# Lower parts of the streamed weights on VectorE instead of GpSimd during a selective scan

## The reference

```python
y_diag = jnp.einsum('bclgn,bcsgn,bgrcls,bcsgrp->bclgrp', Cm, Bm, lmat, x)
states = jnp.einsum('bclgn,bgrcl,bclgrp->bcgrpn', Bm, decay_states, x)
states = jnp.einsum('bgrzc,bcgrpn->bzgrpn', decay_chunk, states)
y_off = jnp.einsum('bclgn,bcgrpn,bgrcl->bclgrp', Cm, prev_states, jnp.exp(a_cum))
```

## Time and profile before

| | us |
|---|---|
| three runs: lowest, median, highest | 2100.3, 2104.06, 2104.97 |
| the profiled execution | 2098.91 |
| its span, first to last instruction | 2097.2 |
| TensorE busy | 1942.2 (93%) |
| GpSimd busy | 961.4 (46%) |
| VectorE busy | 816.4 (39%) |
| ScalarE busy | 705.8 (34%) |
| L697, lower parts on GpSimd, 212 times | 533.7 |
| L943, upper parts on ScalarE, 212 times | 223.9 |

### The profile page before, as it was taken

One profiled execution on the slowest core, in us unless ns is written; L12 is line 12 of the kernel. 1 busy time (PEld: TensorE's weight loads), 2 busy tenths in 40 slices (PEclk: granted clock), 3 DMA queues, 4 the chain that ended last, 5 costly groups with the idle time before them and its releaser, 6 DMA issues. The chain is left out here.

```text
span 2097.2 us, 36461 instructions
## 1 busy us (share of the span) xinstructions
PE 1942.2 (93%) x14668; PEld 1773.5 (85%) x14668; DVE 816.4 (39%) x1567; ACT 705.8 (34%) x1292; POOL 961.4 (46%) x685
## 2 busy tenths in 40 slices
PE   7998899988888998999999999899978899999996
PEld 5987887867778998999998998755548899999996
DVE  7364573746455220022233112378655521012134
ACT  4453553634134221122223131266533322122222
POOL 2445454444447643356444342454403565346552
PEclk9998999989998999999999999799999899999998
DMA  4211312113131226332221333420161122222221
GB/s 163 80 51 41 121 51 111 51 70 127 41 117 62 80 72 172 90 121 82 81 79 51 127 136 109 173 78 1 41 222 41 51 81 90 81 81 80 82 82 64
DMA packets 61077, 185.12 MB, mean 88 GB/s; under 512 B 15519, under 2 KB 20287, under 8 KB 59425
## 3 DMA queue, kind: packets, MB, share of 16 engines
q1 hardware_dynamic: 48720, 130.18, 18.9%
q0 software_dynamic: 9952, 50.08, 6.7%
q10 hardware_dynamic: 2288, 3.23, 0.4%
HBM read 167.05 MB, written 27.35 MB: 93 GB/s over the span
## 5 line engine op out<-in xcount | busy, mean ns | idle before, releaser
L1299 PE MATMUL dense<-xs,split 128*128 128x288 f32 x6848 | 978.3, 301 | 28.2 <-POOL xs L805 8.5
L1299 PEld LDWEIGHTS dense<-xs,split 128*128 128x128 f32 x6848 | 942.0, 192 | 63.2 <-issue 43.5
L697 POOL TENSOR_TENSOR split<-ring,split 128x1024 fp32r<-128x1024 f32 x212 | 533.7, 2518 | 815.7 <-ACT split L943 793.7
L943 ACT ACTIVATE split<-ring 128x1024 fp32r<-128x1024 f32 x212 | 223.9, 1056 | 798.2 <-PE dense L1299 775.4
L1299 PE MATMUL dense<-hid,split 128*128 128x288 f32 x3072 | 415.8, 298 | 5.8 <-POOL split L697 5.8
L1299 PEld LDWEIGHTS dense<-hid,split 128*128 128x128 f32 x3072 | 414.3, 191 | 6.0 <-POOL split L697 6.0
L1863 DVE SCALAR_TENSOR_TENSOR tile<-tile,dense 128x576 f32<-128x576 f32 (+1 forms) x56 | 42.2, 754 | 422.0 <-PE dense L1299 422.0
L2032 DVE TENSOR_SCALAR sq<-dense 128x576 f32<-128x576 f32 x64 | 48.5, 757 | 310.5 <-PE dense L1299 310.5
L914 POOL TENSOR_SCALAR tile<-tile,tile,tile 128x128 f32<-128x128 f32 (+3 forms) x128 | 77.8, 622 | 80.8 <-DVE tile L2195 80.8
L1851 DVE SCALAR_TENSOR_TENSOR tile<-tile,tile,tile 128x512 f32<-128x512 f32 x72 | 87.5, 1215 | 41.2 <-ACT tile L1024 39.4
L816 POOL TENSOR_TENSOR hid<-sq,hid 128x576 f32 x64 | 77.3, 1208 | 0.0
(11 more groups left out here) (316 smaller groups left out, 2118.2 us busy)
## 6 DMA issues: line engine op xcount, KB each, us to landing
ring<-in_w SPq DMA_DIRECT2D x212, 512.0 KB, 3.3
tile<-in_state POOLq DMA_DIRECT2D x4, 2048.0 KB, 9.2
o_sssm<-tile POOLq DMA_DIRECT2D x4, 2048.0 KB, 7.5
tile<-in_cmp POOLq DMA_DIRECT2D x32, 256.0 KB, 3.2
tile<-in_win POOLq DMA_DIRECT2D x8, 1024.0 KB, 5.9
tile<-in_sel SPq DMA_DIRECT2D x32, 256.0 KB, 5.2
o_kv<-tile POOLq DMA_DIRECT2D x1, 3456.0 KB, 12.2
bskew<-bscr SPq DMA_DIRECT2D x1, 3072.0 KB, 22.3
```

Of the source, the lines that this page charges most:

```text
L697: pool.tensor_tensor(split[:, j, 1, :], ring[:, j, :], split[:, j, 0, :].bitcast(F32), ALU.subtract).then_inc(w_split, 1)
L943: act.activation(split[:, j, 0, :], ring[:, j, :], ACT.Copy).then_inc(w_hi, 1)
L1299: mm = pe.matmul(dense[:, 2 * par + h_, 0:HT], split[:, j, w, cols], v[:, kk, h_ * HT:(h_ + 1) * HT], start=kk == 0 and t == 0, stop=kk == ...
```

## The change

In the scan's twenty tiles VectorE makes the lower parts that GpSimd made, 38 of them (slots 12 to 49); before and after the scan GpSimd still makes them. The part for the even slot plus 2 is made behind the convolutions, the norm and the residual and ahead of the wait for `y_done`; the one for the odd slot plus 2 is made in the next tile, behind the masked product L1914 (after the last tile for the last one). VectorE waits once for the twelve parts that GpSimd has made, and GpSimd waits for VectorE's last one before it goes on with parts of its own.

```diff
 # GpSimd, loop over the tiles
                 if n + 1 < len(TILES):
                     segment_rows(*TILES[n + 1])
-                if filler(g, c):
-                    split_lo(filler(g, c)[0] + 2)
                 if c == 3:
...
                     if g + 1 < MG:
                         load_states(g + 1)
-                if filler(g, c):
-                    split_lo(filler(g, c)[1] + 2)
             pool.dma_start(a["o_pssm"], st.rearrange("p g m -> p (g m)")).then_inc(outs, 16)
...
+            pool.wait_ge(w_split, S_OUT[1] + 2)
             finish_los(0)
 # VectorE
+            def split_lo(s):
+                if s == GB + 2:
+                    dve.wait_ge(w_split, s)
+                dve.wait_ge(w_hi, s + 1)
+                j = s % NSLOT
+                dve.tensor_tensor(split[:, j, 1, :], ring[:, j, :], split[:, j, 0, :].bitcast(F32),
+                                  ALU.subtract).then_inc(w_split, 1)
+
+            def split_before(n):
+                if n and filler(*TILES[n - 1][:2]):
+                    split_lo(filler(*TILES[n - 1][:2])[1] + 2)
+
             for g, c, n in TILES:
...
                 dve.tensor_tensor(Gm[0:L, 0:L], bM[0:L, P:P + L], triu[0:L, c // 4, 0:L], ALU.mult
                                   ).then_inc(g_masked, 1)
+                split_before(n)
                 dve.wait_ge(g_masked, n + 1)
...
                     residual(B_OUT[0], 2 * c - 2, ALPHA, filler(g, c)[0] + 1)
+                if filler(g, c):
+                    split_lo(filler(g, c)[0] + 2)
 
                 dve.wait_ge(y_done, n + 1)
...
+            split_before(len(TILES))
             mean_square(MG - 1)
             norm(MG - 1)
```

## The result

The changed kernel took 2066.52 us (median of 4 runs, 2065.07 to 2073.3) beside 2102.18 us for the kernel before (4 runs, 2097.8 to 2104.97): a ratio of 0.9839, 95% interval 0.9818 to 0.9861. It is faster by 35.7 us.

A forecast was written before the change was run, and what follows sets the result against it. TensorE, 93% busy, was taken to wait in the scan for a VectorE chain that GpSimd's lower part lengthened. Terms: 18.6 us of waits plus 6.4 of clock, 25.0, so 2079 us; range 2067 to 2094.

The forecast's parts named there:

- rival B: Scan: the long L1851 isn't the split's doing, VectorE's subtraction just adds to its chain; 12.5 us slower, 2116.5; chance 0.09.
- VectorE's price: Each of the 38 lower parts in the scan takes VectorE 1.22 us, 46 us in sum.
- rival C: Scan: VectorE needs 2.4 us per lower part too; only 4.8 us gained, no clock, 2099 us; chance 0.05.
- Rival A: GpSimd's remaining L687, L688, L756 run earlier and delay the even convolution 1 us; 12.6 us gained, 2091; chance 0.16.
- no L1851 above 2 us: Sign that the forecast is right: no such long convolution step remains anywhere in the scan.
- Six state-add waits: TensorE's ordinary waits for L1957 ahead of the next tile shrink from 2.2 to about 0.6 us: 9.6 us gained.
- Two norm tiles: Their L1957 waits (1.65 us): about 1.5 saved, split costs 1.22; taken as 0, between -1 and +1 us.
- Tiles 16 and 0: Shorter waits of TensorE there, 1.81 and 1.04 us before: about 1.5 and 0.8 us gained.
- L730: Tiles 5, 10, 15: without the odd part ahead, two TensorE waits vanish, the third falls to 2.8: 4.6 us gained.
- L1909: Tiles 17 and 18: TensorE's 3.72 us wait behind the four slow L1898 shrinks; 2.1 us go.
- Last chunks: Tiles 4, 9, 14, 19: even part on the path to L1962 against a shorter L1944; 0, 2 us either side.
- The clock: Tiles 2, 3, 8, 12 regain the clock lost after 2.2 us waits in front: 6.4 us, or 0, or more.

The follow-up runs named there:

- e3: Changed kernel plus two unused GpSimd multiplications that read SBUF, at the even part's old place in all tiles but the last chunks: 2097.29 us, ratio 0.9975.
- e4: Changed kernel plus four unused GpSimd memsets that only write SBUF, at that same old place of the even part: 2069.22 us, ratio 0.9843.
- e9: As e8, with GpSimd's wait for the stored states and the load of the next ones moved behind L730: 2050.57 us, ratio 0.9755.
- e8: Changed kernel with the even part back on GpSimd, behind y's gate (in last chunks behind the eight products); odd part stays on VectorE: 2071.81 us, ratio 0.9843.
- e2: Changed kernel with the even part back on GpSimd at its old place, only the odd part on VectorE: 2093.41 us, ratio 0.9966.

## Why the prediction was right or wrong

**The bound and the mechanism were right.** TensorE did wait for a VectorE chain that the lower part lengthened without being waited for by name. e3 put a reader back and lost the gain, e4 put a writer back and kept it. That settles rival B (the long convolution step has another cause): in tile 1 the second step is 0.75 us with nothing else done to it, and nothing in the result ends on B's side.

**VectorE's price was right:** 1.22 us; 38 parts took 49.0 us in sum, 1.29 each, where 46 were forecast. So rival C is out. Rival A (GpSimd's remaining work in place of the split) is real but mostly covered. The decays times mask (L1919, now L1933) take 36.8 us in sum instead of 26.8. One step of the even convolution is above 2 us (2.82 at 219.70, in tile 5), and two of the odd one are, 2.38 each, in tiles 6 and 11. Yet in the six ordinary tiles the even convolution still waits for ScalarE, 0.57 to 1.70 us, so the slack that was put at 0.4 held. Thus the test "no L1851 above 2 us" was too strict. The prediction also says that the long L1851 and L697 end together; by the earlier trace rows L1851 ends 0.55 us later (130.76 and 130.21), within the 0.75 us that such a step takes by itself.

**The waits, term by term.** Forecast were 18.6 us; idle time fell by 20.0.

- Six state-add waits: 2.22 to 0.38 each, 11.1 us instead of 9.6. The chain was costed with durations where starts count: three pairs take 2.83 us, not 3.0, and the subtraction 1.14, not 1.22.
- Two norm tiles (8 and 13): taken as 0 with a bound of 1 us each way, they wait 2.55 and 2.60 instead of 1.65, near the lower bound. VectorE's part was about right: in tile 13 the multiplies go from 4.56 to 3.00 us with 1.22 behind them. What the sum left out is ScalarE, whose decays the chain hangs on. Its table load ahead of them starts 3.86 us behind the end of the last block (408.64 before, 390.30 after) in both kernels, while TensorE now begins the tile 1.86 us sooner behind that end (before, then after):

```profile
410.87 0.63 PE L1406 MATMUL bXM<-ident,tile 128*128 128x128 f32 x4 [2.23 <-DVE tile L1957]
412.50 1.28 ACT L1071 ACT_TABLE_LOAD   x1
```

```profile
390.67 0.63 PE L1403 MATMUL bXM<-ident,tile 128*128 128x128 f32 x4 [0.37 <-DVE tile L1973]
394.15 1.28 ACT L1068 ACT_TABLE_LOAD   x1
```

  So part of what is saved in front of the tile comes back at its end: from the tile's first matmul to the end of the state add the chain grows from 21.0 to 21.9 us, at a clock of 1.00 in both. In tile 8 it shrinks, from 22.6 to 21.9, but TensorE's own work shrinks more, from 21.10 to 19.53, by the clock.
- Tiles 16 and 0: both waits went whole, 1.81 and 1.04, instead of 1.5 and 0.8.
- L730: 7.4 to 4.8, 2.6 us instead of 4.6. Tile 10's wait (0.66) went, but tile 5's only fell from 1.63 to 1.24, and tile 15's from 5.12 to 3.58, not to 2.8. GpSimd stood longer for the store of the states, 9.34 us instead of 7.43 in tile 5 and 7.34 instead of 6.58 in tile 15. The store was taken as fixed; it varies (in the second profile of the changed kernel tile 5 has 8.35 us, and a wait of 0.23), and e8 shows how far.
- L1909 (now L1922): 4.4 to 2.2, as forecast.
- Last chunks: taken as 0 with 2 us to either side, they gave 3.2 us, 10.7 to 7.5. The two state adds of tile 4 now run back to back, and L1960, which was L1944, has its 0.48 us:

```profile
191.32 0.48 DVE L1960 TENSOR_TENSOR tile<-tile,tile 128x256 f32<-128x256 f32 x1
...
192.91 1.28 DVE L1978 TENSOR_TENSOR tile<-bXM,tile 128x512 f32<-128x512 f32 x2
```

- Not in the sum: waits for the squares grew by 1.6; two smaller ones gave 1.6.

**The clock is the term that was mis-sized:** 6.4 us forecast, 13.7 measured. The four tiles named (2, 3, 8, 12) gave 6.4 to the tenth, each now at 1.00. But tile 9 gave 3.0 more, tile 18 2.6 (19.55 instead of 22.11) and tile 19 1.5. The step that failed is the rule that only a 2.2 us wait in front of a tile costs clock, with the last chunks left as an unpriced "or more". These three have their waits inside: L1909 in tile 18 went from 3.72 to 1.57 us and the clock from 0.87 to 1.00; the state loop in tile 9 was waited for 2.00 us instead of 2.79, and the clock went from 0.76 to 0.84, though the wait in front of that tile grew (2.55 against 1.65). The price was right and the list of places too short. (The rule's counterexamples were misread too: the waits of 2.23 us without a loss stand in front of tiles 7 and 13; tile 6 has 0.94.)

How far this goes, the second profile of the changed kernel tells. There tiles 2, 3, 8, 12, 18 and 19 are at 1.00 again, with the same busy times to 0.1 us. The other last chunks are not the same. With a wait for the state loop of 2.00 us in each, tile 4 takes TensorE 24.63 us at a clock of 1.00 where the first profile has 29.21 at 0.84, tile 9 30.73 instead of 29.29, and tile 14 32.19 instead of 30.64. The matmuls behind that wait, in tiles 4 and 9 of the first profile and then in tile 4 of the second:

```profile
194.24 2.08 PE L1471 MATMUL bXM<-tile,tile 32*128 32x512 f32 x4 [2.00 <-DVE tile L1978]
...
316.37 1.40 PE L1471 MATMUL bXM<-tile,tile 32*128 32x512 f32 x4 [2.00 <-DVE tile L1978]
```

```profile
193.78 1.13 PE L1471 MATMUL bXM<-tile,tile 32*128 32x512 f32 x4 [2.00 <-DVE tile L1978]
```

So the same wait in the same place of the same kernel is followed by a slower clock in one execution and not in another, and tile 9's 3.0 us can't be put down to its shorter wait. What repeats is 10.5 us: the four tiles, 18 and 19. Which idle time decides for the clock in the last chunks stays open.

In sum the stage gave 33.7 us where 25.0 were forecast: 7.3 of the 8.7 missing are clock, 1.4 are waits. That the waits come so near is partly luck, since terms that are off by +1.5, -1.9, -2.0 and +3.2 us cancel. In the second profile the stage takes 456.47 us, 36.3 less than before, 15.7 of them busy time; the medians differ by 35.7.

**On moving work between these two engines** the Trainium skill warns in "Perfetto Trace Analysis", section "Optimizing Scalar/DVE Operations", that it might not help, since they share a port. It helped here, by 1.6%, and e9 says why for the even part: not because VectorE is faster, for GpSimd in a better place does as well, but because the move took a reader away from beside the chain.

## What to carry to other kernels

When an instruction of VectorE takes its own time plus another's, look for a GpSimd instruction that reads SBUF and starts beside it, and ask who waits at the end of that chain; here moving one of them in time was worth more than choosing the faster engine. Before moving it, read what is queued behind the new place, a store and a load above all (e8). Price what a shorter wait gives back in clock for every stretch with idle time in it, inside the tiles too, and read it from more than one execution. Then ask of each wait left what its chain hangs on: what doesn't move with TensorE (here ScalarE's decays) gives part of the saved time back.

## What was not expected of the hardware

- The record that starts first can still be the one that is blocked: L1851 starts 10 ns ahead of L697 and takes 2.96 us; in e2, where GpSimd's part (130.42) starts 80 ns behind a convolution step (130.34), that step keeps 0.75 us, GpSimd's part takes 2.92, and the next step 2.42.
- GpSimd instructions in a row can hold one VectorE instruction through several of them: in the kernel before one L1851 takes 5.57 us, from 225.12, while GpSimd runs L730, L687, L688 and L697 from 224.34 to 230.14.
- GpSimd waited 6.5 to 13.4 us for the store of the states to land, a transfer of the same size each time: 6.47 to 7.43 in the kernel before, 7.28 to 9.34 in the changed one, 10.29 to 13.40 in e8.
- Of 33.7 us in the stage, 13.7 came back as clock and not as wait; and two executions of the same changed kernel differ in tile 4 alone by 4.6 us of TensorE's busy time, at equal waits.
